# State products of two sample streams in two row halves of the array, their parts laid out through memory

## The chip, the core and the metric

The kernel is one program on one core of a Trainium2 chip. The metric is the device time of one execution in microseconds (us), lower is better. TensorE is the matrix engine (PE; its weight loads are listed as PEld), VectorE is DVE, ScalarE is ACT, GpSimd is POOL, and SyncE (SP) only issues transfers here. Products go to PSUM, which the kernel uses as 8 banks of 128 x 512 numbers.

## The reference, cut to what matters

One layer of a streaming encoder: a half-step FFN, a mixer (short convolution, and retention with four heads), a second half-step FFN. It runs over 512 frames of one new stream and over 16 frames of each of 8 running streams ("sample streams"). The part that the change touches is the new state of each sample stream: for each head, S_new = decay * S + k^T v, where k is 16 frames x 256, v is 16 frames x 512 and S is 256 x 512.

```python
k_dec = k * jnp.exp(lg[None, :] * (L - 1.0 - idx[:, None]))[None, :, :, None]
S_new = jnp.exp(lg * L)[None, :, None, None] * S + jnp.einsum('blhd,blhe->bhde', k_dec, v)
```

## The kernel before

Products are made in float32r from a high and a low part of each operand, in three products: low x high, high x low, high x high. The 640 rows of activations (512 new, 128 sample) run as tiles of 128. Each engine has its program in order; semaphores tie them together. PSUM banks are handed out round robin: `bank(n)` on PE waits until the banks that it will write have been freed (`psum_free`, counted up by DVE or ACT when they have read a bank), and `psum_full` tells the readers.

A head (`head(i)` on each engine, i = 0 to 3) is, on PE: the v and k projections (`natural(4, ...)`), transposes of the rotated keys, scores, `cross(0)` (products of a query with the old states, in four column groups of the array), the output tiles, a gate unit (`unit_of_chunk`), transposes of the normalised output, `cross(1)`, the new state of the long stream, the transposes of the sample rows (banks from U_T5 on), and then the state products of the sample streams in three places: `state_products(1, (0, 1))` ahead of the output projection, `state_products(1, (2, 3))` after its first quarter (m = 0), and `state_products(0, range(4))` at its end, right ahead of the next head's projections. I call the three places A, B and C.

The sample keys of all 8 streams are one tile of 128 rows (16 rows a stream), with parts k4h and k4l; the values are v4h and v4l. ACT copies them into `vp` and `kp` (`pack`, lines 1618 to 1622): group g of four holds two streams, in rows 0 to 31 the high part, 32 to 63 one low part, 64 to 95 the high part again, so that one product of 96 rows gives all three. Rows 96 to 127 are zeroed once (lines 2271, 2272). As one group holds two streams, ACT makes for each stream a copy `km` of the keys with the other stream's rows set to zero (`masked_keys`, lines 1624 to 1629, factor `odd_even`), four ahead of place A and four behind place B. A stream takes two products of 128 x 128 by 128 x 512 (`state_products`, lines 1237 to 1246), 16 in a head.

The order of the work around it. DVE: the gated output of the sample rows (`gated(4)`, `gated(5)`) frees the last two of the banks that the output projection's `bank(4)` at m = 0 waits for; `new_state` (line 2394) adds each product to the state and frees its bank; `branch(m)` takes the output projection's banks. ACT: after `kd` it packs, waits for `packed`, makes the gate's sigmoid, `gated_hi`, the root of the variance. SP (`head_loads`, line 658): after `cross(0)` it loads the second four states into `state`, waits for `packed`, and loads `swish` into `sg`, whose memory v4h and v4l share; DVE's `gated(0)` waits for that load. After it come the next weight chunks. POOL loads the high parts of weight chunks and splits off the low ones.

Of the kernel before, what the change touches and what calls it, by code (L numbers as in the profile page):

```python
# [8 lines left out]
NP, NS_, TS = 512, 8, 16  # L9
# [160 lines left out]

HT_S, HT_M, HT_Q, HT_K, HT_G, HT_W = 0, 512, 640, 768, 773, 776
# [121 lines left out]
def build_layer(nc, a):  # L293
# [3 lines left out]
    with ctx:  # L297
# [3 lines left out]
        def sem(name):  # L301
            return ctx.enter_context(nc.semaphore(name))
# [18 lines left out]
        odd_even = sb("odd_even", [128, 2])  # L321
# [7 lines left out]
        slab = (nc.sbuf_base + 31) // 32 * 32  # L329
        end = nc.sbuf_base + nc.sbuf_bytes_remaining  # L330
# [69 lines left out]
        km = hm.take("km", [128, 4, DK], f32r)  # L400
        SC0 = [0, 512, 896, 1152, 1280]
        rot_at = hm.at
# [77 lines left out]
        packed = sem("packed")  # L480
        keys_masked = sem("keys_masked")
# [81 lines left out]
        def _(sync):  # L563
# [94 lines left out]
            def head_loads(i):  # L658
# [5 lines left out]
                sync.wait_ge(packed, i * 24 + 12)  # L664
                sync.dma_start(sg[:, 0:SWISH_TILES, :], a["swish"][i]).then_inc(swish_in, 16)
# [146 lines left out]
        def _(pe):  # L812
            ck, bk, hr, zr, hd, kc = (Count() for _ in range(6))
# [423 lines left out]
            def state_products(group, slots):  # L1237

                for bb in slots:
                    kc.add()  # L1240
                    pe.wait_ge(keys_masked, kc())
                    for d in range(2):
                        b = bank()
                        last = mm(ps[:, b, :], km[:, bb, d * 128:(d + 1) * 128],
                                  vp[:, (4 * group + bb) // 2, :], True, True)
                    last.then_inc(psum_full, 2)
# [19 lines left out]
            def head(i):  # L1266
# [48 lines left out]
                state_products(1, (0, 1))  # L1315
                assert bk.at - u0 == U_OUT

                for m in range(4):
# [11 lines left out]
                    if m == 0:  # L1330
                        state_products(1, (2, 3))
                state_products(0, range(4))
# [12 lines left out]
            pe.wait_ge(consts_in, 32)  # L1345
# [12 lines left out]
        def _(act):  # L1358
# [49 lines left out]
            def window(ffn):  # L1408
# [25 lines left out]
                if ffn == 0:  # L1434
                    act.dma_start(ident[:, :], a["ident"]).then_inc(consts_in, 16)
                    act.dma_start(odd_even[:, :], a["odd_even"]).then_inc(consts_in, 16)
# [129 lines left out]
            act.wait_ge(consts_in, 32)  # L1566

# [50 lines left out]
            def pack(out, n, part):  # L1618

                for g in range(4):  # L1620
                    copy(out[32 * n:32 * n + 32, g, :], part[32 * g:32 * g + 32, :].bitcast(f32)
                         ).then_inc(packed, 1)

            def masked_keys(group):

# [13 lines left out]
            def head(i):  # L1639
# [46 lines left out]
                for n in range(4):  # L1686
                    gated_hi(n)
# [925 lines left out]
```

## Time and profile before

| | us |
|---|---|
| median of 3 runs | 1798.13 |
| the 3 runs | 1797.13 to 1800.16 |
| the profiled execution | 1800.08 |
| its span | 1798.3 |
| PE busy in the span | 1775.9 (99%) |
| DVE, ACT, POOL busy | 1282.8, 647.9, 547.0 |
| TensorE clock granted, mean | 0.998 |

The four heads run from about 943 to 1296 us of the span. In a timeline row the first number is the start, the second the time from the start of the first to the end of the last of the instructions merged in it. Products overlap in the records: a product of 128 x 512 is listed with 0.39 us, but in a dense row one starts every 0.227 us, and this pitch is what it costs.

### The profile page before, as it was taken

Reading aid. Unit: us, or ns where it says so; the run is one execution under the profiler, and the core shown is the slowest. Engines: PE = TensorE matmul, PEld = TensorE weight load, DVE = VectorE, ACT = ScalarE, POOL = GpSimd, SP = SyncE. Lnnn points to the kernel's source line nnn. Section 1 sums busy time; section 2 is a strip of 40 time slices with the busy share of each in tenths; the row PEclk is TensorE's granted clock in tenths of the full one; section 3 lists DMA queues with packets and bytes.
Section 4 is the critical chain, followed back from the end, with each engine's and each line's share of the span. In section 5 each row is a group of like instructions: output and inputs, shape, how many; then the busy total and the mean of one; then the engine's idle time right before and its main releaser. Section 6 shows DMA issues by size and latency. Waiting matters only on the chain.

```text
span 1798.3 us, 26938 instructions
## 1 busy us (share of the span) xinstructions
PE 1775.9 (99%) x10852; PEld 1654.3 (92%) x10852; DVE 1282.8 (71%) x1694; ACT 647.9 (36%) x1105; POOL 547.0 (30%) x361
## 2 busy tenths in 40 slices
PE   9999999999999999999999999999999999999997
PEld 8989999898999999999998979797988989899895
DVE  7958485678788787776257666767867958485675
ACT  5425233242545454543106050504224425243242
POOL 2424242242232222221341323232243324233231
PEclk9999999999999999999999999999999999999999
DMA  7442424324443343432864959586972342423313
GB/s 272 132 138 71 141 79 133 119 94 175 147 147 126 112 138 98 141 102 76 292 225 153 338 187 328 189 296 233 345 273 95 129 141 71 139 73 129 128 48 105
DMA packets 88986, 285.74 MB, mean 159 GB/s; under 512 B 8736, under 2 KB 11168, under 8 KB 88608
## 3 DMA queue, kind: packets, MB, share of 16 engines
q1 hardware_dynamic: 48176, 171.72, 28.9%
q0 software_dynamic: 15120, 55.06, 9.1%
q10 hardware_dynamic: 25568, 57.26, 8.7%
q8 instruction: 86, 1.41, 0.3%
q14 instruction: 36, 0.29, 0.1%
HBM read 242.78 MB, written 42.28 MB: 159 GB/s over the span
## 4 chain that ended last, share of the span: by engine, by line
PE 96%; DVE 1%; DMA 1%; issue 1%; ACT 0%; POOL 0%; DVEq 0%; SPq 0%; POOLq 0%; ACTq 0%
PE ps L818 95%; PE ps L1227 1%; DMA wh<-in_weights 1%; PE ps L1136 0%; DMA raw<-in_weights 0%; DVE y L2192 0%; POOL wl L720 0%; ACT xh L1367 0%; DVE ct L1795 0%; DVE z L2181 0%; DVE y L2201 0%; DVE hl L1795 0%; DVE wl L1795 0%; ACT hh L1367 0%; DVE rt L1795 0%
## 5 line engine op out<-in xcount | busy, mean ns | idle before, releaser
L818 PE MATMUL ps<-th,wql 128*128 128x320 f32 x1136 | 350.9, 309 | 0.0
L818 PE MATMUL ps<-th,wqh 128*128 128x320 f32 x1136 | 350.7, 309 | 0.0
L818 PE MATMUL ps<-tl,wqh 128*128 128x320 f32 x1136 | 350.1, 308 | 0.0
L720 POOL TENSOR_TENSOR wl<-raw,wh 128x1024 fp32r<-128x1024 f32 x101 | 259.8, 2573 | 104.0 <-DMA wh<-in_weights 69.1
L1367 ACT ACTIVATE pu<-ps 128x320 f32<-128x320 f32 x213 | 93.3, 438 | 526.4 <-PE ps L818 526.3
L1795 DVE TENSOR_TENSOR wql<-qraw,wqh 128x512 fp32r<-128x512 f32 x213 | 263.3, 1236 | 17.3 <-ACT wqh L1367 17.1
L818 PE MATMUL ps<-xl,wqh 128*128 128x320 f32 x852 | 262.7, 308 | 0.0
L818 PE MATMUL ps<-xh,wqh 128*128 128x320 f32 x852 | 262.7, 308 | 0.0
L818 PE MATMUL ps<-xh,wql 128*128 128x320 f32 x852 | 262.6, 308 | 0.0
L733 POOL TENSOR_TENSOR quad_s<-qraw 128x512 f32<-128x512 f32 x71 | 93.6, 1318 | 473.1 <-DVE wql L1795 425.9
L1795 DVE TENSOR_TENSOR wql<-quad_s,wqh 128x512 fp32r<-128x512 f32 (+1 forms) x213 | 194.2, 912 | 46.1 <-ACT wqh L1367 45.3
L708 POOL DMA_DIRECT2D wh<-in_weights x99 | 55.7, 563 | 525.0 <-PE ps L818 419.8
L818 PEld LDWEIGHTS ps<-tl,wqh 128*128 128x128 f32 x1136 | 213.3, 188 | 0.4
L818 PEld LDWEIGHTS ps<-th,wql 128*128 128x128 f32 x1136 | 213.2, 188 | 0.4
L818 PEld LDWEIGHTS ps<-th,wqh 128*128 128x128 f32 x1136 | 213.3, 188 | 0.0
L1367 ACT ACTIVATE wqh<-quad_s 128x512 fp32r<-128x512 f32 (+1 forms) x213 | 163.7, 769 | 50.2 <-PE ps L818 50.2
L818 PE MATMUL ps<-wh,hl 128*128 128x512 f32 x430 | 168.3, 391 | 2.0 <-issue 1.4
L818 PE MATMUL ps<-wh,hh 128*128 128x512 f32 x430 | 167.6, 390 | 0.0
L818 PE MATMUL ps<-wl,hh 128*128 128x512 f32 x430 | 167.6, 390 | 0.0
L818 PEld LDWEIGHTS ps<-xh,wql 128*128 128x128 f32 x852 | 159.9, 188 | 0.6 <-issue 0.2
L818 PEld LDWEIGHTS ps<-xl,wqh 128*128 128x128 f32 x852 | 160.0, 188 | 0.4
L818 PEld LDWEIGHTS ps<-xh,wqh 128*128 128x128 f32 x852 | 160.0, 188 | 0.0
(224 smaller groups left out, 3429.7 us busy)
## 6 DMA issues: line engine op xcount, KB each, us to landing
qraw<-in_quads SPq DMA_DIRECT2D x142, 512.0 KB, 3.7
raw<-in_weights SPq DMA_DIRECT2D x105, 512.0 KB, 3.8
wh<-in_weights POOLq DMA_DIRECT2D x99, 512.0 KB, 5.2
state<-in_state_ret ACTq DMA_DIRECT2D x32, 512.0 KB, 7.1
out_ret_sample<-state ACTq DMA_DIRECT2D x32, 512.0 KB, 4.5
state<-in_state_ret SPq DMA_DIRECT2D x16, 512.0 KB, 5.4
qk_scratch<-ctp SPq DMA_DIRECT2D x8, 640.0 KB, 5.5
swish_scratch<-ctp SPq DMA_DIRECT2D x6, 640.0 KB, 3.0
```

Source lines behind the costliest of these rows:

```text
L708: pool.dma_start(w_hi(r), a["weights"][c]).then_inc(hi_loaded[r], 16)
L720: pool.tensor_tensor(w_lo(r), w_raw(r), w_hi(r).bitcast(f32), ALU.subtract).then_inc(chunk_split, 1)
L733: pool.tensor_tensor(qs[:, 0, :], qraw[:, c0, 512:1024], qraw[:, c1, 512:1024], ALU.add).then_inc(pool_sums, 1)
L818: ins = nc.tensor.matmul(out, lhs, rhs, start=start, stop=stop, skip_group_check=adds)
L1227: last = nc.tensor.transpose(cols(k, 128, ps[:, b, :]), src, ident[:, :])
L1367: return nc.scalar.activation(out, in_, ACT.Copy, **kw)
L1795: return V.tensor_tensor(out, x, y, op)
```

## The change

The state products of a group g now run from `vp` and `kp` themselves, without a mask. The two streams of a group no longer lie interleaved: the even stream's three parts of 16 rows fill rows 0 to 47, the odd stream's rows 64 to 111. A product has 48 rows, in the lower or upper half of the array. The count stays at 16 a head, each with 128 x 512 results, in the order even, odd for each half d of the keys. A call does one group and takes its four banks at once. The places stay: g = 2 at A, g = 3 at B, g = 0 and 1 at C.

As no engine but a transfer moves rows freely, the parts go through memory: ACT issues six transfers a head, which store v4h, v4l, v4h and k4h, k4h, k4l into `packed_values` and `packed_keys` (16-row blocks side by side for each stream); SP issues four that load them into the two halves of `vp` and `kp`. The 24 copies of `pack`, the 8 of `masked_keys`, the table `odd_even` and the two memsets go. PE waits for the loads, ACT and SP for the stores. `slab` is padded so that its distance to `xh` stays at three quarters of LEVEL, and the buffers behind `kp` move.

```diff
+PACKED, PACK_STORES, PACK_LOADS = 3 * TS, 16 * 3, 16 * 2
...
-        odd_even = sb("odd_even", [128, 2])
...
+        slab += (3 * LEVEL // 4 - (slab - xh_at)) % LEVEL
...
-        km = hm.take("km", [128, 4, DK], f32r)
+        hm.at = max(hm.at, sums_at + 8 * KT * NT)
...
-                sync.wait_ge(packed, i * 24 + 12)
-                sync.dma_start(sg[:, 0:SWISH_TILES, :], a["swish"][i]).then_inc(swish_in, 16)
+                for out, of, saved, done in ((vp, "packed_values", values_saved, values_packed),
+                                             (kp, "packed_keys", keys_saved, keys_packed)):
+                    sync.wait_ge(saved, PACK_STORES * (i + 1))
+                    for odd in range(2):
+                        sync.dma_start(out[64 * odd:64 * odd + PACKED, :, :].bitcast(f32),
+                                       a[of].rearrange("(g o) p d -> o p g d", o=2)[odd]).then_inc(done, 16)
+                    if out is kp:
+                        continue
+                    sync.dma_start(sg[:, 0:SWISH_TILES, :], a["swish"][i]).then_inc(swish_in, 16)
...
-            def state_products(group, slots):
-
-                for bb in slots:
-                    kc.add()
-                    pe.wait_ge(keys_masked, kc())
-                    for d in range(2):
-                        b = bank()
-                        last = mm(ps[:, b, :], km[:, bb, d * 128:(d + 1) * 128],
-                                  vp[:, (4 * group + bb) // 2, :], True, True)
-                    last.then_inc(psum_full, 2)
+            def state_products(i, g):
+
+                b0 = bk.at
+                bank(4)
+                pe.wait_ge(values_packed, PACK_LOADS * (i + 1))
+                pe.wait_ge(keys_packed, PACK_LOADS * (i + 1))
+                for d in range(2):
+                    for odd in range(2):
+                        rows = slice(64 * odd, 64 * odd + PACKED)
+                        last = mm(ps[:, (b0 + 2 * odd + d) % 8, :], kp[rows, g, d * 128:(d + 1) * 128],
+                                  vp[rows, g, :], True, True)
+                last.then_inc(psum_full, 4)
...
-                state_products(1, (0, 1))
+                state_products(i, 2)
...
-                        state_products(1, (2, 3))
-                state_products(0, range(4))
+                        state_products(i, 3)
+                for g in range(2):
+                    state_products(i, g)
...
-            def pack(out, n, part):
-
-                for g in range(4):
-                    copy(out[32 * n:32 * n + 32, g, :], part[32 * g:32 * g + 32, :].bitcast(f32)
-                         ).then_inc(packed, 1)
-
-            def masked_keys(group):
-
-                for bb in range(4):
-                    st = 4 * group + bb
-                    copy(km[:, bb, :], kp[:, st // 2, :].bitcast(f32),
-                         scale=odd_even[:, st % 2:st % 2 + 1]).then_inc(keys_masked, 1)
+            def save_packed(out, parts, saved):
+
+                for n, part in enumerate(parts):
+                    act.dma_start(out[:, TS * n:TS * n + TS, :], part[:, :].bitcast(f32)).then_inc(saved, 16)
...
-                pack(vp, 0, v4[0])
-                pack(vp, 1, v4[1])
-                pack(vp, 2, v4[0])
+                if i:
+                    act.wait_ge(values_packed, PACK_LOADS * i)
+                save_packed(a["packed_values"], (v4[0], v4[1], v4[0]), values_saved)
                 act.wait_ge(k4_made, i + 1)
-                pack(kp, 0, k4[0])
-                pack(kp, 1, k4[0])
-                pack(kp, 2, k4[1])
+                if i:
+                    act.wait_ge(keys_packed, PACK_LOADS * i)
+                save_packed(a["packed_keys"], (k4[0], k4[0], k4[1]), keys_saved)
...
-                act.wait_ge(packed, i * 24 + 12)
+                act.wait_ge(values_saved, PACK_STORES * (i + 1))
...
+                act.wait_ge(keys_saved, PACK_STORES * (i + 1))
                 for n in range(4):
                     gated_hi(n)
                 roots(5, 6)
-                act.wait_ge(packed, i * 24 + 24)
-                masked_keys(1)
...
-                act.wait_ge(psum_full, u0 + U_S1B + 4)
-                masked_keys(0)
...
-            step(V.memset(vp[96:128, :, :].bitcast(f32), 0.0))
-            step(V.memset(kp[96:128, :, :].bitcast(f32), 0.0))
```

## Rows read from the trace of the kernel before

**Rows 1.** The page: the chain that ended last, by engine.
```profile
PE 96%; DVE 1%; DMA 1%; issue 1%; ACT 0%; POOL 0%; DVEq 0%; SPq 0%; POOLq 0%; ACTq 0%
```

**Rows 2.** Groups by line and shape (busy us, mean ns | idle before): state products.
```profile
L818 PE MATMUL ps<-vp,km 128*128 128x512 f32 x64 | 17.1, 399 | 0.0
```

**Rows 3.** Timeline of PE and DVE at place A, first head.
```profile
982.84 1.17 PE L818 MATMUL ps<-vp,km 128*128 128x512 f32 x4
983.05 0.74 DVE L1795 TENSOR_TENSOR ogt<-ps,sg 128x256 f32<-128x256 f32 x2
...
983.89 0.39 PE L818 MATMUL ps<-ogh,wl 128*128 128x320 f32 x1
```

**Rows 4.** Timeline of PE at place B, first head.
```profile
991.01 1.09 PE L818 MATMUL ps<-vp,km 128*128 128x512 f32 x4
991.94 0.31 PE L818 MATMUL ps<-ogh,wl 128*128 128x320 f32 x1
```

**Rows 5.** Timeline of PE and DVE at place C, first head.
```profile
1013.06 2.02 PE L818 MATMUL ps<-vp,km 128*128 128x512 f32 x8
1013.33 0.82 DVE L2409 COPY z<-ps 128x640 f32<-128x640 f32 x1 [1.35 <-PE ps L818]
...
1014.07 2.06 DVE L2400 SCALAR_TENSOR_TENSOR state<-state,ht,ps 128x512 f32<-128x512 f32 x3
...
1014.95 0.47 PE L818 MATMUL ps<-wh,xl 128*128 128x512 f32 x1
```

**Rows 6.** Timeline of PE around the first head's first `cross`, in four column groups.
```profile
954.72 0.28 PE L818 MATMUL ps<-ql,kh 128*128 128x256 f32 x1
954.84 0.28 PE L818 MATMUL ps<-qh,kh 128*128 128x256 f32 x1
955.04 1.92 PE L818 MATMUL ps<-state,qx 128*32 128x512 f32 x16
956.79 1.04 PE L818 MATMUL ps<-vs,sc 128*32 128x512 f32 x8
957.76 0.50 PE L818 MATMUL ps<-vh,scl 128*128 128x512 f32 x1
958.09 0.39 PE L818 MATMUL ps<-vl,sch 128*128 128x512 f32 x1
```

**Rows 7.** Timelines of ACT and DVE, first head, from packing to the gate.
```profile
951.98 2.58 ACT L1367 ACTIVATE vp<-v4h 32x512 fp32r<-32x512 f32 x4
...
968.48 1.28 ACT L1674 ACT_TABLE_LOAD   x1 [1.88 <-PE ps L818]
...
956.96 0.42 DVE L1795 TENSOR_TENSOR k4l<-kd,k4h 128x256 fp32r<-128x256 f32 x1
...
972.83 1.28 DVE L1795 TENSOR_TENSOR ogt<-ps,sg 128x512 f32<-128x512 f32 x2
```

**Rows 8.** Timeline of SP's queue, first head.
```profile
957.89 1.92 SPq L662 DMA_DIRECT2D state<-in_state_ret  x4
959.85 0.75 SPq L665 DMA_DIRECT2D sg<-swish_scratch  x1
972.05 41.76 SPq L571 DMA_DIRECT2D raw<-in_weights  x5
```

**Rows 9.** Transfers of the stretch 950 to 985 us, 40 slices; landing in us.
```profile
GB/s 169 257 407 346 19 0 0 0 0 0 56 220 389 396 403 403 413 417 430 334 80 0 9 0 0 0 122 248 403 365 61 0 0 0 0 0 0 0 0 0
...
sg<-swish_scratch SPq DMA_DIRECT2D x1, 960.0 KB, 10.3
```

**Rows 10.** Last head: SP's queue, DVE, and the transfer in 1237 to 1257.
```profile
1240.87 0.47 SPq L665 DMA_DIRECT2D sg<-swish_scratch  x1
...
1253.85 1.28 DVE L1795 TENSOR_TENSOR ogt<-ps,sg 128x512 f32<-128x512 f32 x2
...
sg<-swish_scratch SPq DMA_DIRECT2D x1, 960.0 KB, 9.4
```

**Rows 11.** The page: small stores to memory, issue to landing.
```profile
out_y_sample<-y SPq DMA_DIRECT2D x2, 256.0 KB, 3.2
```

More of the change, by code:

```diff
@@ L479, in build_layer @@
         head_ready = sem("head_ready")
-        packed = sem("packed")
-        keys_masked = sem("keys_masked")
+        values_saved, keys_saved = sem("values_saved"), sem("keys_saved")
+        values_packed, keys_packed = sem("values_packed"), sem("keys_packed")
         swish_sig_made, swish_made, swish_in, k4_made = (
@@ L812, in _ @@
         def _(pe):
-            ck, bk, hr, zr, hd, kc = (Count() for _ in range(6))
+            ck, bk, hr, zr, hd = (Count() for _ in range(5))
             owed = [False]
@@ L1344, in _ @@
             ffn(True)
-            pe.wait_ge(consts_in, 32)
+            pe.wait_ge(consts_in, 16)
             begin_stage()
@@ L1435, in window @@
                     act.dma_start(ident[:, :], a["ident"]).then_inc(consts_in, 16)
-                    act.dma_start(odd_even[:, :], a["odd_even"]).then_inc(consts_in, 16)
                     act.dma_start(convw[:, :, :], a["conv_w"]).then_inc(cache_in, 16)
@@ L1565, in _ @@
             roots_and_to_T(1)
-            act.wait_ge(consts_in, 32)
             def state_load(i):
@@ L2589 @@
         "ident": np.eye(128, dtype=np.float32),
-        "odd_even": ((np.arange(128)[:, None] // TS % 2 == np.arange(2)[None, :])
-                     & (np.arange(128)[:, None] < 96)).astype(np.float32),
     }
@@ L2603 @@
     for name, shape in (("qk", (H, 2, 128, 2, NT)), ("swish", (H, 128, SWISH_TILES, NT)), ("gate_c", (128, KT, NT)), ("gate_r", (128, KT, NT)),
-                        ("mix", (128, KT, NT))):
+                        ("mix", (128, KT, NT)), ("packed_values", (NS_, PACKED, DV)), ("packed_keys", (NS_, PACKED, DK))):
         args[name] = nc.dram_tensor(f"{name}_scratch", shape, mybir.dt.float32, kind="Internal").ap()
```

## The prediction

> **What bounds the kernel now.** I read the chain first: TensorE carries 96% of it [rows 1]. So a saving counts only where PE starts its next product earlier, and a cost only where PE is made to wait. ACT, which the change relieves of 32 copies a head, is not on the chain, and I give that relief nothing. Next the group of the products that change: 64, no idle time ahead of them [rows 2]. Then the timeline at the three places of a head, to see what releases the work that follows.
>
> Place A: four products start at 982.84; the output projection starts at 983.89 [rows 3]. At the dense pitch of 0.227 us four would end at 983.75. The rest is a wait for DVE: it needs the banks that `gated(4)` and `gated(5)` free, and these two run from 983.05 to 983.79. DVE sets that start.
>
> Place B: 991.01 to 991.94 is 0.93 us for four, 4 x 0.227 = 0.91 and no wait [rows 4]. PE sets it.
>
> Place C: eight from 1013.06, the next head's first product at 1014.95 [rows 5]. Eight pitches are 1.82, to 1014.88. The first bank of the next head must be freed by DVE: `branch(7)` runs 1013.33 to 1014.15, and the first of the three state updates of 2.06 us ends at about 1014.07 + 0.74 = 1014.81; a semaphore's tenth later is 1014.92. PE and DVE end there together. The other three heads repeat this to within 0.05 us, as they do at A and B.
>
> **The change, part by part.**
>
> The pairs. Two products in different row halves ought to run side by side. The trace has no row halves, but it has column quarters: 24 products of `cross`, each listed at 0.59 us, start 16 of them in 956.79 - 955.04 = 1.75 us, four each 0.44 us [rows 6]. Four quarters overlap fully there. So I take a pair at one pitch of 0.227; the bounds are 0.22 (a quarter product's 0.109 twice) and 0.454 (one behind the other).
>
> The switch of the array's shape. Around `cross`: the score product before it starts at 954.84, pitch 0.12, so the next was due at 954.96 and came at 955.04: 0.08. After it, the second four of `vs,sc` began at 957.22 and were due to hand over at 957.66; the next came at 957.76, and its successor 0.33 later where 0.227 is usual: 0.10 + 0.10 [rows 6]. I take 0.28 for a visit; the bounds are 0 and 0.56 (a row switch twice as dear). The Trainium skill (TensorEngine Tiling, Key Properties) says that changing the tiling mode drains the engine; the trace agrees with these 0.28 us. By that page's speedup of up to two, without its drain, place B would gain 0.45 instead of what follows.
>
> Place A: 982.84 + 0.08 + 2 x 0.227 + 0.10 = 983.48, before the 983.86 at which DVE lets the projection go. Gain 0. All of the saved time becomes wait.
>
> Place B: 0.08 + 0.454 + 0.20 = 0.73 against 0.93: gain 0.20, bounds +0.48 (no switch cost) and -0.08 (double). `bank(4)` here wants two banks more at once, those of the first two streams' state; DVE updates that state right after place A, some 7 us of projection earlier, so they are free.
>
> Place C: group 0 ends at about 1013.06 + 0.08 + 0.45 = 1013.6. Group 1 takes its four banks at once, so it waits for `branch(7)`, 1014.15 + 0.07 = 1014.22, where before only its last stream did. It ends at 1014.22 + 0.45 + 0.10 = 1014.77, and the next head still waits for DVE until 1014.92. Gain 0, cover left 0.15. With that cover gone each 0.1 us more costs 0.4 in the sum.
>
> Transfers instead of copies. Values are stored from 951.98 on, three issues of 256 KB [rows 7]; 256 KB land in 3.2 us elsewhere [rows 11], so all are in memory near 957.5, before SP has issued its state loads (957.89 to 959.81) [rows 8]. Keys are ready when k4l is made, 957.38 [rows 7], and land some 5 us later. ACT's two new waits end long before the gate (968.48) and `gated_hi`, which follows `gated(0)` at 972.83 [rows 7]; behind them only these two wait. SP's wait for the keys has the next weight load behind it, issued at 972.05 in any case [rows 8]. The loads of `kp` queue behind `sg` and should land near 974, 8 us before PE asks.
>
> What is not free is that `sg` now stands behind the loads of `vp` in SP's queue. In the first head it is issued at 959.85 and lands 10.3 later, at 970.15 [rows 8, 9]; DVE needs it at 972.83 [rows 7]. Margin 2.7 us. In the last head 1240.87 + 9.4 = 1250.3 against 1253.85: 3.6 [rows 10]; the middle two have 4.2. The stretch moves 403 GB/s when full [rows 9]; ahead of `sg` now come 0.79 MB of `vp` and, on ACT's queue, up to 0.39 MB of keys: 1.18 MB / 403 GB/s = 2.9 us. So `sg` is late by 0.2 us in the first head and in time in the others. From `gated(0)` to place A, DVE is busy nearly without a gap and PE waits for it, so what is late there is paid in full. Bounds: 0 (the keys use the idle stretch before 959) and 1.8 in all (0.4 MB/us plus one more issue of 0.75 us: 3.9 us late gives 1.2 + 0.3 + small ones).
>
> Addresses: `slab` stays at its level; `sc`, `on`, `rot` move 1184 bytes down, level 0 instead of 160. 64 `vs,sc` products see that. I take 0, bounds +-0.6 us (0.01 us each). Both memsets lie in a stretch where DVE waits for PE: 0.
>
> Sum: 4 x (0 - 0.20 + 0) + 0.2 = -0.6 us. The profiled execution took 1800.08 (span 1798.3 and 1.8 around it), so it would be 1799.5. It stands 1.95 above the median of the three; against the median, which is what will be compared, 1798.13 - 0.6 = **1797.5 us**.
>
> **The rivals.**
>
> R1, the halves do not run side by side, so that the change does not do what it says. Then A ends 982.84 + 0.08 + 0.91 + 0.10 = 983.93, +0.07; B 1.19 against 0.93, +0.26; C 1014.22 + 0.91 + 0.10 = 1015.23, +0.31. That is 0.64 a head, 2.6 in four, with `sg` 2.8: 1800.9. For it: no row product in the trace. Against it: the column quarters, whose weight loads start together too.
>
> R2, slower: the swish load becomes the bound. Place: SP's queue ahead of `gated(0)`. With a delay d in each head, the loss is (d - 2.7) + 2 (d - 4.2) + (d - 3.6); it makes the kernel slower by 0.2% from d = 4.75 on. At d = 5.4 it is 6.9 less 0.8: 1804.2. For that the new transfers would have to cost nearly twice their bytes at 403 GB/s, or the values' stores would have to land after SP asks at 959.8. The Trainium skill (DMA: Bandwidth & Descriptors, Why a DMA increments its semaphore by 16) says that a transfer uses only as many engines as divide both slowest dimensions: 8 streams against 128 partitions gives 8 of 16 engines for the six stores. No row before the change has such a store. What speaks for R2 in rows is the margin of 2.7 us only.
>
> R3, DVE's hold at A and C is softer than I read it, and the pairs count everywhere: 32 pitches of 0.227 less 12 visits of 0.28, -3.9: 1794.2. Against it: both holds are dependences in the code with ends that match within 0.1 us.
>
> **How the numbers follow.** Forecast 0.62, R1 0.14, R2 0.10, R3 0.05; the remaining 0.09 I leave to what I have not seen (addresses, transfers that collide elsewhere), two thirds of it slower. The measurement tells about 0.2% from no change, 3.6 us. Forecast and R1 are inside it, R2 above 1801.7, R3 at its edge. Faster 0.06, same 0.81, slower 0.13. The runs alone spread by 1.5 us around their middle; the range takes in the forecast, its bounds (-1.9 to +2.1 with place B's and the load's ends) and R1: 1795.2 to 1801.4.
>
> **What would show it.** In the profile after: pairs of products starting within a few hundredths in A, B and C (if one starts each 0.227, R1); B's first product to the next projection's 0.73; an unchanged 1.05 at A and 1.89 at C with the wait put down to DVE; `sg` landing about 2.9 us later after its turn; no PE wait for `vp` or `kp`. A DVE wait for `sg` ahead of `gated(0)` of more than a few tenths in every head would be R2. The prediction is wrong if a head gains or loses more than 0.9 us, or if something outside the heads moves by more than 1 us.

## The result and the profile after

The kernel after takes 1821.65 us (median of 4 runs, 1820.46 to 1825.82) beside 1798.68 for the kernel before on the same chip (4 runs, 1797.13 to 1800.16). The ratio is 1.0129, 95% interval 1.0117 to 1.0141: slower by 1.3%, where 1797.5 was forecast and 1801.4 was the top of the range. Its span is 1819.0 us, 20.7 more than before, and the mean granted clock 0.995 (0.998 before). Medians and ratios here and below are of runs near full clock: two of e16's ten runs (1935 and 2498 us, at granted clocks of 0.85 and 0.65) are left out.

The page of the kernel after, the chain by engine and TensorE's busy time, to be held against [rows 1]:

```profile
PE 82%; issue 5%; DMA 4%; DVE 3%; POOL 2%; SPq 1%; ACT 0%; DVEq 0%; POOLq 0%; ACTq 0%
PE 1780.5 (98%) x10852; PEld 1652.5 (91%) x10852; DVE 1285.2 (71%) x1692; ACT 585.3 (32%) x977; POOL 547.5 (30%) x361
```

TensorE has fallen from 96% of the chain to 82%, and transfers with their issues have taken most of the difference. The answer for the tile `sg` (what its engine sat idle for, us and times, and the time from issue to landing) and TensorE's waits (total, times, longest) say which transfer:

```profile
  DMA sg<-swish_scratch: 19.4, 4
...
DMA to landing us min/median/max: 13.8/16.2/17.7
```

```profile
PE ps L1235 <- DVE on L2270: 16.3, 4, 5.9
```

DVE waits once a head for the load of `swish`, 19.4 us in all, and TensorE then waits for DVE's normalised output, 16.3 us in all. Before, this load landed in 8.2 to 10.3 us and DVE never waited for it. DVE's timeline at `gated(0)` in the first three heads shows the size of each wait, in brackets:

```profile
978.40 1.29 DVE L1792 TENSOR_TENSOR ogt<-ps,sg 128x512 f32<-128x512 f32 x2 [4.66 <-DMA sg<-swish_scratch]
...
1079.96 1.29 DVE L1792 TENSOR_TENSOR ogt<-ps,sg 128x512 f32<-128x512 f32 x2 [6.68 <-DMA sg<-swish_scratch]
...
1177.62 1.29 DVE L1792 TENSOR_TENSOR ogt<-ps,sg 128x512 f32<-128x512 f32 x2 [3.47 <-DMA sg<-swish_scratch]
```

The last head's is 4.6. The first transpose of the rotated keys in each head slips against before by 0.8, 5.8, 13.5 and 16.1 us, and the stage behind the heads by 21.3. So the four heads lose 5.0, 7.7, 2.7 and 5.1, 20.5 in all; 0.8 is lost ahead of them and 0.6 regained behind.

TensorE idles for 16.3 of these 20.5 us; DVE makes up for some 0.8 of each of its own waits before TensorE needs it. The other 4.2 us go with TensorE's clock. Its wait in the second head, and then, for each head, the stretch from the first transpose behind the wait (`ident,on`) to the first product of the output projection; the third number from the end is the granted clock:

```profile
1088.30 1.97 PE L1235 MATMUL ps<-ident,on 128*128 128x128 f32 x8 [5.91 <-DVE on L2270]
...
986.74:989.75 3.01, 3.01 (x12) 2.03 (x12) 2.43 (x6) 0.83 (x2) 0.00 (x0) 0.51 0.00 0
1088.30:1091.35 3.05, 3.05 (x12) 2.07 (x12) 2.46 (x6) 0.83 (x2) 0.00 (x0) 0.50 0.00 0
1185.96:1187.86 1.90, 1.76 (x12) 1.18 (x13) 1.80 (x4) 0.40 (x2) 0.00 (x0) 1.00 0.00 0
1283.06:1285.45 2.39, 2.39 (x12) 1.41 (x13) 2.24 (x6) 0.75 (x2) 0.00 (x0) 0.65 0.99 401
```

Before, the stretch took 1.90 us in every head, at a clock of 1.00. In the first, second and fourth head, ahead of which TensorE had idled 3.88, 5.91 and 3.85 us, the clock fell to its lower level of 1.2 GHz (0.50) for all or part of the stretch, which took 3.01, 3.05 and 2.39 us: 2.7 us lost. In the third, after an idle time of 2.67 us, it stayed at 2.4 GHz and nothing was lost. The remaining 1.4 us or so are what is left over; the projection's products right behind account for them at least in part: in the second head they start each 0.27 us up to 1092.6, where 0.15 is usual. In e1, e4, e11, e16 and e18 below, in whose profiled heads no wait for `sg` is over 1.2 us, the clock stays at its full level through all four heads.

SP's queue in the first head, after (start, time to the end of the last issue):

```profile
958.71 2.21 SPq L663 DMA_DIRECT2D state<-in_state_ret  x4
960.96 1.31 SPq L669 DMA_DIRECT2D vp<-packed_values_scratch  x2
962.31 0.51 SPq L673 DMA_DIRECT2D sg<-swish_scratch  x1
...
966.89 0.80 SPq L669 DMA_DIRECT2D kp<-packed_keys_scratch  x2
```

Against [rows 8] `sg` is issued 2.5 us later: 0.8 because the state loads start later, most of the rest for the two new issues. It then lands 16.1 us after its issue where it took 10.3 [rows 9]. These 5.8 us are the part that has to be explained. The transfers of 950 to 985 us, after (40 slices of 0.875 us, issues with their landing):

```profile
GB/s 0 154 342 398 321 119 157 115 166 169 143 104 276 366 397 377 394 408 371 166 178 273 255 297 201 197 183 232 200 315 315 286 225 220 210 98 5 0 0 0
...
sg<-swish_scratch SPq DMA_DIRECT2D x1, 960.0 KB, 16.1
vp<-packed_values_scratch SPq DMA_DIRECT2D x2, 384.0 KB, 11.5
```

Two stretches are slow. From 954.4 to 960.5 us, slices 6 to 12, the stores run at 104 to 169 GB/s in a stretch that was empty before. From 966.6 us on, the 20th slice, `vp` comes in: 166 and 178 GB/s, and not over 315 from there to the end, where the kernel before moved 403 to 430. In the records of the single packets a 2 KB packet takes 84 ns up to 966 us and 130 to 200 after it, and `swish`'s packets of 7.5 KB take 492 ns on average in the four heads, 297 before. From 966.6 us on the engines are listed as full; each packet takes longer.

TensorE's side, first head, place B (after):

```profile
996.97 0.30 PE L826 MATMUL ps<-ogh,wh 128*128 128x320 f32 x1
997.20 0.73 PE L826 MATMUL ps<-vp,kp 48*128 48x512 f32 x4
997.86 0.41 PE L826 MATMUL ps<-ogh,wl 128*128 128x320 f32 x1
998.12 0.31 PE L826 MATMUL ps<-ogl,wh 128*128 128x320 f32 x1
```

and place C:

```profile
1018.95 0.31 PE L826 MATMUL ps<-ogh,wh 128*128 128x320 f32 x1
1019.18 0.73 PE L826 MATMUL ps<-vp,kp 48*128 48x512 f32 x4
1020.24 0.73 PE L826 MATMUL ps<-vp,kp 48*128 48x512 f32 x4 [0.32 <-DVE z L2404]
1020.99 0.47 PE L826 MATMUL ps<-wh,xl 128*128 128x512 f32 x1
```

Four products take 0.66 us to their successor at B (0.93 before, [rows 4]): pairs do run side by side. At C the second four wait for DVE, and the last product ahead of them to the next head's first is 2.04 us, as before. At both places the four products take what was forecast to within 0.1 us; what the switch of shape costs behind them is weighed under e7 and e8. The 23 us are lost in the transfers.

### The profile page after: what moved, and what is told of

It reads as the page before. It is cut to its first block, busy times and chain, and to the rows that moved or that the text cites. A ratio compares the mean times of both kernels' runs of the same rounds, so it can differ in the third digit from the quotient of the medians.

```text
span 1819.0 us, 26808 instructions
## 1 busy us (share of the span) xinstructions
PE 1780.5 (98%) x10852; PEld 1652.5 (91%) x10852; DVE 1285.2 (71%) x1692; ACT 585.3 (32%) x977; POOL 547.5 (30%) x361
## 4 chain that ended last, share of the span: by engine, by line
PE 82%; issue 5%; DMA 4%; DVE 3%; POOL 2%; SPq 1%; ACT 0%; DVEq 0%; POOLq 0%; ACTq 0%
PE ps L826 82%; DMA sg<-swish_scratch 3%; POOL wl L728 2%; DMA wh<-in_weights 1%; DVE ogl L1792 0%; PE ps L1235 0%; PE ps L1144 0%; DVE z L1792 0%; SPq L663 0%; POOL wh L716 0%; DVE y L2189 0%; ACT xh L1378 0%; DVE ogt L1792 0%; DVE ct L1792 0%; DVE z L2178 0%
```

## The experiments

Diffs are against the kernel after unless said. The kernel before ran beside each: 1798.60 (e1 to e4), 1799.38 (e5 to e8), 1798.97 (e9 to e11), 1798.84 (e12 to e14), 1798.47 (e15 to e18).

### Is it the queue's order, the loads or the stores?

**e1: `swish` ahead of the loads.**

```diff
+                sync.wait_ge(values_saved, PACK_STORES * (i + 1))
+                sync.dma_start(sg[:, 0:SWISH_TILES, :], a["swish"][i]).then_inc(swish_in, 16)
                 for out, of, saved, done in ((vp, "packed_values", values_saved, values_packed),
...
-                    sync.dma_start(sg[:, 0:SWISH_TILES, :], a["swish"][i]).then_inc(swish_in, 16)
```

> The changed kernel with one edit: SP issues the swish load ahead of the loads of vp and kp instead of between them. My theory now: nearly all of the 20.7 us in the span is DVE waiting for sg ahead of gated(0), 19.4 us in four waits, and PE after it. Then sg lands within 12 us of its issue at about 961, DVE waits under 1 us in all, and the time is 1797 to 1801. Rival: the product halves or the new waits on PE cost something of their own, or the later loads of kp only move the wait: then it stays above 1805.

1800.40 us, ratio 1.0006 (0.9997 to 1.0016), `sg` waits 1.4 us in two heads. The transfers of 950 to 985 in e1:

```profile
GB/s 37 164 379 435 227 159 166 150 190 176 62 229 254 364 390 394 404 434 419 437 400 180 154 238 236 180 185 198 158 149 288 193 276 229 98 0 0 0 0 0
```

The loss is gone, so it came through the wait for `sg` alone. The slow stretch is not gone: it now stands behind `swish`, at 149 to 288 GB/s, with `vp` and `kp` in it and nobody waiting. The loads themselves are slow, not `swish` behind them.

**e2 and e3: one side left out after the first head.**

```diff
-                    for odd in range(2):
+                    for odd in range(2 if i == 0 else 0):
```

```diff
-                save_packed(a["packed_values"], (v4[0], v4[1], v4[0]), values_saved)
+                if i == 0:
+                    save_packed(a["packed_values"], (v4[0], v4[1], v4[0]), values_saved)
```

> Left out: in heads 1 to 3 the loads of vp and kp; their products use head 0's values. The six stores of each head stay. If the stores are what holds sg up (8 of 16 engines busy with them up to 959.7 us, then keys beside the state loads): sg still lands 13 us or more after its issue in heads 1 to 3 and the time stays above 1812. If the loads are: DVE waits some 5 us for sg in head 0 and under 1 us in the others, 1801 to 1806.

> Left out: in heads 1 to 3 the six stores; the loads of vp and kp stay and read what head 0 stored. If the loads hold sg up: sg lands 14 us or more after its issue in heads 1 to 3, DVE waits 3 to 6 us a head, 1814 to 1821. If the stores do: a wait in head 0 alone, 1801 to 1806.

e2, without loads in heads 1 to 3: 1806.66 us, 1.0032 (1.0018 to 1.0045); `sg` waits once, 4.0 us in the first head, and lands in 9.8 and 9.9 us in the others. Its runs spread from 1802.41 to 1807.37, and the profiled one, with a span of 1800.6, is among the shortest; so I read from it where it waits, not how much is left. e3, without stores in heads 1 to 3: 1811.52, 1.0063 (1.0046 to 1.0080), waits 13.6 us, among them 5.22 and 2.05 in the heads without stores. In the profiled execution stores alone delay nothing; its median says that typical runs lose some 4 us more, and no trace shows where. Loads alone cost most of it: 9.2 us of waits in heads 1 to 3, where the kernel after has 14.8.

**e6: stores on all engines.** The six stores write one block of 128 rows each, in place of 8 streams x 16 rows.

```diff
-                    act.dma_start(out[:, TS * n:TS * n + TS, :], part[:, :].bitcast(f32)).then_inc(saved, 16)
+                    act.dma_start(out.rearrange("s p d -> (s p) d")[128 * n:128 * n + 128, :], part[:, :].bitcast(f32)).then_inc(saved, 16)
```

> The changed kernel, but each of the six stores writes its 128 rows to 128 rows of memory side by side, so that nothing in its shape is 8; the loads are unchanged and so bring rows that are not theirs. If the stores ran on 8 of 16 engines (share 0.47 and 160 GB/s from 954 to 959 us): they finish in half the time and the key stores no longer load one half of the engines; then sg lands 1 to 3 us earlier than in the changed kernel, 1810 to 1817. If the stores cost only their bytes: no change, 1820 to 1823.

1811.65 us, 1.0071 (1.0056 to 1.0086). The transfers of 950 to 985 in e6:

```profile
GB/s 0 131 318 332 344 377 405 190 0 0 169 229 138 384 403 405 412 405 391 204 150 152 180 198 171 361 404 293 174 232 281 346 375 56 23 0 0 0 0 0
```

The stores now run at 318 to 405 GB/s and are through by 957, where the kernel after had them at 104 to 169 until 960. So half of the engines is what they use there: in the records of after the 16 engines are busy 0.47 on average while the values are stored. The Trainium skill (DMA: Bandwidth & Descriptors, Why a DMA increments its semaphore by 16) gives 8 of 16 engines for this shape; these runs agree. The loads that follow are as slow as before (150 to 204). Waits for `sg` come to 8.8 us in three heads, and in the first DVE starts at 977.23, just as `sg` lands, after 3.5 us put down to a product that had long ended: 12.3. The half stores thus take some 10 us of the 23, but only together with the slow loads: with them the four state loads land in a median of 8.0 us in that stretch instead of 5.7 in e6, which eats into the margin of 2.7 to 4.2 us that hides the stores in e2.

### What makes the loads slow?

**e4: the same bytes into 128 partitions.** As many bytes, packets and issues, the products read what lies in their rows.

```diff
-                        sync.dma_start(out[64 * odd:64 * odd + PACKED, :, :].bitcast(f32),
-                                       a[of].rearrange("(g o) p d -> o p g d", o=2)[odd]).then_inc(done, 16)
+                        sync.dma_start(out[:, (0, 1)[odd]:(1, 3)[odd], :].bitcast(f32),
+                                       a[of].rearrange("s p d -> (s p) d").rearrange("(g q) d -> q g d", q=128)[:, (0, 1)[odd]:(1, 3)[odd], :]).then_inc(done, 16)
```

> The loads of vp and kp move the same bytes in the same 2 KB and 1 KB rows from the same stores, but into 128 partitions (3 groups) instead of 48 at a time; the products read rows that are not theirs. If the loads are slow because each is packed into 48 partitions (the 2 KB packets took 130 to 204 ns from 966 us on, against 85 ns for those of the state loads): packets at 85 ns again, sg lands 10 to 12 us after its issue, 1798 to 1804. If they are slow because of what they read (rows just written to memory, a stride between groups) or because of the stores: no change, 1815 to 1822.

1799.61 us, 1.0003 (0.9993 to 1.0012), no wait for `sg`, landing 10.3 to 10.7. The transfers of 950 to 985 in e4:

```profile
GB/s 94 229 407 379 197 180 190 199 176 47 102 266 236 372 377 392 407 397 407 417 431 408 376 379 200 170 98 314 389 365 33 0 0 0 0 0 0 0 0 0
```

Slices 19 to 22 now hold 407 to 431 GB/s. The whole loss is gone with the stores as they were: it is the shape of the loads.

**e5, e9, e10: 48 rows spread out, sixteen rows apart and together.**

```diff
-                        sync.dma_start(out[64 * odd:64 * odd + PACKED, :, :].bitcast(f32),
+                        sync.dma_start(out[odd:odd + 2 * PACKED - 1:2, :, :].bitcast(f32),
```

```diff
+                    for n in range(6):
...
+                        sync.dma_start(out[n:n + 121:8, :, :].bitcast(f32),
...
+                        sync.dma_start(out[16 * n:16 * n + 16, :, :].bitcast(f32),
```

(the last two lines are e9's and e10's)

> The changed kernel, each load of vp and kp still 48 partitions from the same rows of memory in the same order, but into every second partition (0, 2, .. 94 and 1, 3, .. 95) instead of 48 in a row; rows 96 to 127 zeroed once; the products read rows that are not theirs. If what is slow is the crowding of the writes into 48 neighbouring partitions: the 2 KB packets fall from some 150 to 220 ns to about 90, sg lands 10 to 12 us after its issue, 1798 to 1803. If it is what the loads read in memory, or that a load has only 48 partitions: unchanged, 1815 to 1822.

> The changed kernel with each of vp and kp loaded by six transfers of 16 partitions, eight apart (n, n + 8, ... n + 120), the same bytes from the same rows; vp and kp zeroed once; the products read rows that are not theirs. Theory: a load's rate goes with how many groups of 8 neighbouring partitions it writes: 48 in a row touch 6 of 16 (in the run with the swish load first they ran alone at about 140 GB/s, against 390 to 400 of full ones), 48 of 96 touch 12 (about 290). So here, 16 of 16, the packets stay near 85 to 95 ns; sg is issued 2 to 3 us later for the four more issues and lands some 10 us after, DVE waits 0 to 2 us a head, 1799 to 1806. Rival: small loads are slow because they have few partitions: then worse than the changed kernel, over 1825.

> The same as e9_sixteen_apart but each transfer into 16 neighbouring partitions (16n to 16n + 15), 2 groups of 8 of 16. Theory: the 0.79 MB of vp move at some 50 GB/s, 15 us instead of 2, sg lands 25 us or so after its issue and DVE waits some 10 us a head: 1835 to 1865. Rival: as in e9 the number of transfers or of partitions is what counts, and the two runs take the same time.

e5: 1811.15 us, 1.0060 (1.0040 to 1.0080), waits 8.8 (its runs spread from 1804.23 to 1813.05, and the profiled one took 1806.77). e9: 1814.11, 1.0083 (1.0069 to 1.0097), waits 13.0. e10: 1836.31, 1.0208 (1.0194 to 1.0222), waits 31.1. The transfers of 950 to 985 in e10:

```profile
GB/s 56 206 445 407 178 183 190 171 159 101 74 242 307 400 363 394 404 403 206 143 112 117 225 138 155 173 134 142 136 140 342 172 180 226 268 346 263 118 187 28
```

Same rows, same issues, and e10 loses 22 us more than e9: where the partitions lie decides. Spreading them does not restore the pace either: e9 shows 194 to 245 GB/s in slices 19 to 22, and its packets of 2 KB take 157 ns at 967 to 968 us. But its 13 us are not all pace. Its six issues put `sg` into the queue 2.6 to 3.3 us later in a head than the two of e4 do, and outside the first head `sg` then lands 10.6 to 11.5 us after its issue, nearly as in e4. My expectation for e9 (1799 to 1806) was missed by 8 us, and I could not say from these three whether it is crowding, or few partitions, or both.

**e12 to e14: the order of the rows in memory.** e12 fills 128 partitions from rows that lie close together in memory, e13 the 48 partitions of the kernel after and e14 the sixteen apart of e9 from rows that lie far from each other.

```diff
+                                       a[of].rearrange("s p d -> (s p) d").rearrange("(g j e) d -> g e j d", e=16, j=8)[g]
...
+                                       a[of].rearrange("s p d -> (s p) d").rearrange("(p g o) d -> o p g d", g=4, o=2)[odd]).then_inc(done, 16)
...
+                                       a[of].rearrange("s p d -> (s p) d").rearrange("(p g n) d -> n p g d", g=4, n=6)[n]
```

> The wide loads of e4 (128 partitions, 3 groups), but the rows of memory are dealt so that the 16 engines read neighbouring rows, 2 KB apart, instead of each its own block of 16 KB; one transfer a group. If only the destination counts: 1798 to 1803, packets near 90 ns. If the closeness of the rows read counts: packets of 120 ns and more, 1806 to 1816.

> The changed kernel's loads into 48 partitions in a row, twice, but each partition's four rows lie in a block of eight rows of its own, so that neighbouring engines read 48 KB apart. If the rows read count: sg lands some 3 us earlier than in the changed kernel, 1808 to 1815. If only the destination counts: 1818 to 1823.

> e9 (sixteen partitions eight apart, six transfers), but the 16 engines read rows 48 KB apart instead of 2 KB. If the rows read are what kept e9 slow: packets near 90 ns, 1800 to 1806. If not: 1812 to 1816 as e9, and then what e9 shares with e5 and not with e4 is the small number of partitions.

e13: 1823.01 us, 1.0134 (1.0119 to 1.0149), waits 19.7, as the kernel after. e14: 1811.62, 1.0077 (1.0062 to 1.0092), waits 11.7, near e9. e12: 1802.02, 1.0019 (1.0009 to 1.0028), waits 5.2; its slices 19 to 22 hold 273 to 327 GB/s, and its packets of 2 KB take 103 ns at 967 to 968 us, 85 in e4. So reading rows that lie close together costs a little, and reading them far apart wins back nothing of the 23 us.

**e15 to e18: sets of partitions.** Here I formed the theory that comes nearest: the 128 partitions fall into 16 sets of 8, each set four neighbours and the four that lie 32 above them; a transfer goes at the pace of its fullest set. The Trainium skill (SBUF — State Buffer, Door 1: The DMA port swizzle) describes such sets as ports. e15 and e16 have equal issues, partitions and packets, e17 and e18 are the same block of 64 neighbours with another start.

```diff
+                    for n in range(3):
+                        sync.dma_start(out[(0, 1, 64)[n]:(63, 64, 127)[n]:2, :, :].bitcast(f32),
...
+                        sync.dma_start(out[n:n + 125:4, :, :].bitcast(f32),
...
+                    sync.dma_start(out[0:64, :, :].bitcast(f32),
...
+                    sync.dma_start(out[32:96, :, :].bitcast(f32),
```

(one line of destination each, for e15, e16, e17 and e18)

> The values and the keys are loaded in three transfers each, of 32 partitions and all four column blocks: rows 0, 2, .. 62, then 1, 3, .. 63, then 64, 66, .. 126. The products read what lies in their rows, so the new states are not those of the reference; bytes, packets and products are as many as in the kernel after. Theory of sets: the 128 partitions form 16 sets of 8 (four neighbours and the four 32 above them), each with a sixteenth of the 400 GB/s that full stretches show, and a transfer lasts as long as its fullest set. It gives for the 48 neighbouring rows of the kernel after 8 of 48 rows in the fullest set, 150 GB/s (seen: 166 to 178 at first), for every second of 96 rows 4 of 48, 300 (seen: 235 to 317), for sixteen rows 8 apart 2 of 16, 200, for sixteen together 4 of 16, 100 (seen with two in flight: 112 to 173). Here 4 of 32 rows: 200 GB/s, though no two rows of a transfer are neighbours. Swish waits 9 to 15 us, time 1808 to 1815. Neighbourhood: like e5_spread_rows or better, waits 6 to 9 us, since the rows lie as far apart as there. Number of partitions: fewer than 48, so waits over 9 us here and as many in e16. The Trainium skill (SBUF - State Buffer, Door 1: The DMA port swizzle) describes such sets as ports.

> As e15_second_of_half, but the three transfers take every fourth partition of all 128: rows 0, 4, .. 124, then 1, 5, .. 125, then 2, 6, .. 126. The new states are not those of the reference here either. Theory of sets: 2 of 32 rows in each of the 16 sets, 400 GB/s as for a load into 128 partitions; what is left is the third issue, so as e12_wide_close_rows: swish waits 0 to 5 us, time 1798.5 to 1802.5. Neighbourhood: between e5_spread_rows (every second) and e9_sixteen_apart (every eighth), waits 8 to 13 us, 1809 to 1814. Number of partitions: as e15, over 9 us.

> The values and the keys are loaded in one transfer each, into 64 neighbouring partitions from 0 on, four column blocks: two thirds of the bytes of the kernel after, and the new states are not those of the reference. Theory of sets: 8 of 64 rows in the fullest set, 200 GB/s, so 512 KB take 2.6 us where they would take 1.3 at 400; packets of 2 KB take about twice the 85 ns that they take in the state loads. Swish lands 1.3 us or more later than in e18; waits of a few tenths to 2 us in the first head, time 1798.5 to 1803. Neighbourhood and number of partitions: no difference from e18 in packets, rate or landing.

> As e17_sixty_four_from_0, but the block of 64 neighbouring partitions begins at 32; the new states are not those of the reference. Theory of sets: 32 to 63 fill eight sets with four rows each, 64 to 95 the eight others: 4 of 64 rows, 400 GB/s, packets of 2 KB near 85 to 100 ns, swish lands 1.3 us or more earlier than in e17 and no wait; time 1797.5 to 1800.5. Neighbourhood and number of partitions: as e17 in all.

e15: 1829.83 us, 1.0174 (1.0159 to 1.0189). e16: 1799.98, 1.0009 (0.9999 to 1.0019). e17: 1821.25, 1.0127 (1.0112 to 1.0142). e18: 1799.32, 1.0005 (0.9996 to 1.0015). The transfers of 950 to 985 and what waited for `sg`, e15:

```profile
GB/s 89 206 398 379 199 176 150 171 185 138 78 234 303 400 369 396 399 407 180 140 138 154 221 219 193 208 156 172 294 166 191 203 255 263 318 233 180 66 5 0
...
  DMA sg<-swish_scratch: 25.7, 4
```

e16, where nothing waited for `sg`:

```profile
GB/s 37 220 384 393 234 159 173 190 192 112 57 214 248 356 362 372 376 410 396 414 418 421 408 376 246 198 124 164 370 435 173 0 0 0 0 0 0 0 0 0
```

e17:

```profile
GB/s 0 178 300 407 314 176 183 157 187 169 57 147 282 365 376 356 400 403 350 147 145 147 203 276 200 252 280 157 142 322 300 231 276 215 84 0 0 0 0 0
...
  DMA sg<-swish_scratch: 17.4, 4
```

e18, again without a wait:

```profile
GB/s 23 206 342 398 279 173 194 185 190 96 50 180 277 403 361 365 392 399 384 434 387 434 368 270 179 16 33 197 346 407 215 0 0 0 0 0 0 0 0 0
```

The reader looks at slices 19 to 22 in each. Sixty-four neighbours from 0 run at 145 to 147 GB/s once the stretch has turned, sixty-four from 32 at 384 to 434. Every second partition of a half is as slow as neighbours are (138 to 180), every fourth of all 128 runs at 396 to 421. Neither neighbourhood nor number does that: e15 is spread and slow, e18 is crowded and fast, and both pairs have equal numbers. In the packet records of 967 to 968 us, 2 KB take 254 ns in e15, 243 in e17, 84 in e16 and 89 in e18.

All the loads of the study in this light, with the rate by sets of a full 400 GB/s:

| loads | rows in the fullest set | GB/s by sets | GB/s seen, first slices | ratio |
|---|---|---|---|---|
| e10, 16 together | 4 of 16 | 100 | 112 to 143 | 1.0208 |
| after, 48 in a row | 8 of 48 | 150 | 166 to 178 | 1.0129 |
| e13, 48 in a row, far rows | 8 of 48 | 150 | 169 to 194 | 1.0134 |
| e15, second of half | 4 of 32 | 200 | 138 to 154 | 1.0174 |
| e17, 64 from 0 | 8 of 64 | 200 | 145 to 147 | 1.0127 |
| e9, 16 apart | 2 of 16 | 200 | 194 to 245 | 1.0083 |
| e14, 16 apart, far rows | 2 of 16 | 200 | 206 to 318 | 1.0077 |
| e5, second of 96 | 4 of 48 | 300 | 235 to 246 | 1.0060 |
| e16, every fourth | 2 of 32 | 400 | 396 to 421 | 1.0009 |
| e18, 64 from 32 | 4 of 64 | 400 | 384 to 434 | 1.0005 |
| e4, 128 | 8 of 128 | 400 | 407 to 431 | 1.0003 |
| e12, 128, close rows | 8 of 128 | 400 | 273 to 327 | 1.0019 |

The loads that fill all 16 sets alike are the fast ones, e12 being slowed by the rows that it reads. The fullest set does not give the pace, nor even the order: e15 and e17, put at 200 GB/s, run at 138 to 154, below the 48 in a row that are put at 150, and my expectations of them (up to 1815 and 1803) were missed by 15 and 18 us. The ratios hold more than the pace, since the issues and TensorE's clock add to them: in e15, as in e10, the clock is at 1.2 GHz for 6.8 us in each head. What is shown is that the same bytes in as many packets are fast when they are shared out over all the sets and slow when they lie in half of them. Why half of the sets gives a third of the pace and not half stays open, and that a set is made of four neighbours was not varied by itself.

### TensorE's ledger

**e7 and e8**, on e4, where no wait for `sg` blurs it: all products in rows 0 to 47 (none side by side), and products over all 128 rows (no switch).

```diff
-                        rows = slice(64 * odd, 64 * odd + PACKED)
+                        rows = slice(0, PACKED)
```

```diff
+                        rows = slice(0, 128)
```

> The run with the wide loads (transfers out of the way), but all state products read rows 0 to 47, so that no two lie in different halves. If pairs in different halves overlap: here four products take 4 x 0.227 instead of 2 x 0.227, so place B takes some 0.45 us more, A about 0.1 more, C 0.4 more, 3 to 4 us in all against the wide loads (1799.6), 1802 to 1804. If they never overlapped: the same time as the wide loads to 0.5 us.

> The run with the wide loads, but all state products read all 128 rows: no row halves, no switch of the array's shape, four banks at once as in the change. Against e7_same_half this is the price of the switch: place B 0.93 us as before the change and no gap of 0.2 us around it; place C still waits for DVE before its second four. I expect 0.2 to 0.3 us less than same_half in each of the places that PE sets, 1800 to 1802.5.

e7: 1804.25 us, 1.0029 (1.0019 to 1.0039). e8: 1800.26, 1.0005 (0.9995 to 1.0014). TensorE at place B in e4, in halves:

```profile
991.09 0.30 PE L826 MATMUL ps<-ogh,wh 128*128 128x320 f32 x1
991.33 0.73 PE L826 MATMUL ps<-vp,kp 48*128 48x512 f32 x4
991.99 0.41 PE L826 MATMUL ps<-ogh,wl 128*128 128x320 f32 x1
992.24 0.31 PE L826 MATMUL ps<-ogl,wh 128*128 128x320 f32 x1
```

in e7, one half:

```profile
991.56 0.30 PE L826 MATMUL ps<-ogh,wh 128*128 128x320 f32 x1
991.79 1.19 PE L826 MATMUL ps<-vp,kp 48*128 48x512 f32 x4
992.91 0.41 PE L826 MATMUL ps<-ogh,wl 128*128 128x320 f32 x1
```

and in e8, all rows:

```profile
990.82 0.31 PE L826 MATMUL ps<-ogh,wh 128*128 128x320 f32 x1
990.97 1.08 PE L826 MATMUL ps<-vp,kp 128*128 128x512 f32 x4
991.89 0.31 PE L826 MATMUL ps<-ogh,wl 128*128 128x320 f32 x1
992.03 0.31 PE L826 MATMUL ps<-ogl,wh 128*128 128x320 f32 x1
```

From the last product ahead to the first behind: 0.90 in halves, 1.35 in one half, 1.07 without a switch. So pairing saves 1.35 - 0.90 = 0.45, two pitches of 0.227, and the switch costs 1.35 - 1.07 = 0.28. One more piece shows a row later: the successor comes after 0.25 us in halves, after 0.14 in e8 (992.24 - 991.99 and 992.03 - 991.89). With these 0.11 place B gains 1.07 - 0.90 - 0.11 = 0.06 us a head.

**e11: a version for use.** Streams padded to 64 rows in memory, so that one load fills 128 partitions, and `swish` ahead of it. (`stored(i)` counts one more store in the first head, which fills the padding.)

```diff
+                    sync.dma_start(out[:, :, :].bitcast(f32),
+                                   a[of].rearrange("(g o) p d -> (o p) g d", o=2)).then_inc(done, 16)
...
-                        ("mix", (128, KT, NT)), ("packed_values", (NS_, PACKED, DV)), ("packed_keys", (NS_, PACKED, DK))):
+                        ("mix", (128, KT, NT)), ("packed_values", (NS_, ROWS_KEPT, DV)), ("packed_keys", (NS_, ROWS_KEPT, DK))):
```

> A correct version that takes both findings: each stream's rows in memory are padded from 48 to 64, so that vp and kp are each loaded by one transfer into all 128 partitions (a third more bytes; the padding is stored once), and SP issues the swish load ahead of them. Theory: sg lands 10 to 11 us after its issue, DVE waits nowhere, what is left is the gain of the halves at place B, 0.06 us a head: 1797 to 1800, not to be told from before. Rival: the stores on half of the engines and the extra bytes still cost 1 us or more.

1799.23 us, 1.0003 (0.9994 to 1.0012), no wait for `sg`, landing 9.7 to 10.5. The change can be had without its loss, but there is nothing under it to win.

## Why the prediction was wrong

**The step that failed** is the price of what stands ahead of `sg`: "1.18 MB / 403 GB/s = 2.9 us". The 403 was read from a stretch in which every transfer fills all 128 partitions [rows 9], and it was applied to loads of 48 and to stores by half of the engines, of which the trace had no row. The loads moved at 166 to 178 GB/s. In the first head `sg` landed at 962.31 + 16.1 = 978.4, 8.3 us later than before, not 2.9. The bound I gave, one more issue and 0.4 MB/us, was no bound (and its terms give 3.7 us, not 3.9): it held the rate fixed, and the rate was the unknown. The stores were mis-sized in the same way: "all are in memory near 957.5" came from another store's 3.2 us, and here the stretch of the stores lasts to 960.5 at 104 to 169 GB/s.

**R2 is what happened.** Its place, its formula and its sign were right: with d = 8.3 it gives (8.3 - 2.7) + 2 (8.3 - 4.2) + (8.3 - 3.6) = 18.5 us, and DVE waited 19.4. That they agree so well is partly luck. The 8.3 us are the first head's and hold 0.8 us by which the whole kernel was already late; counted from the start of its own head, `sg` was late by 7.4, 10.9, 7.7 and 8.2 us, each head's wait plus its margin. And the formula charges the wait to TensorE in full and its clock at nothing: TensorE idled 16.3 us, and its lower clock in three heads cost 4.2 more. Its chance of 0.10 and its example of d = 5.4 were too low. The rule that I named beside it, half of the engines for the stores, agrees with the rows and yet is the lesser half: it explains none of the waits alone (e2's profiled execution), and some 10 us beside the loads (e6 against after). What mattered, the sets of partitions that a load fills, I did not weigh.

**The margins** of 2.7, 4.2, 4.2 and 3.6 us were read right and are why the costs do not add: of the 7.4 to 10.9 us in a head 3.5 to 6.7 show as a wait.

**Pairs**: a pair was put at one pitch of 0.227, and four products save two pitches, 0.45, shown by e7 against e4. **R1** did not happen; made on purpose it costs 4 to 5 us against e4 (1.0029 against 1.0003), where the sum had 2.6 + 0.8. By rows of a head against e4: at A 2.15 instead of 1.90 from the transposes to the projection, 0.25 where I had 0.07; at B 0.45, or 0.28 against the kernel before, where I had 0.26; at C 2.43 instead of 2.04, 0.39 where I had 0.31. That is 1.09, four times 4.4.

**The switch**: 0.28 around the visit, as forecast, and 0.11 more on the product behind the first successor. Place B gains 0.06 a head and not 0.20. This was mis-sized by 0.14 a head, 0.6 in the kernel, too little to be seen in a time.

**Place A** gains nothing: 1.90 us from the transposes to the projection in before, e4, e8 and the one head of after in which the clock did not fall. **Place C** gains nothing: 2.04 in before and after, with the wait for DVE where it was forecast, ahead of the second four. In e8, whose products take the old time but in the new grouping of banks, the same distance is 2.33, and the product behind comes 0.08 us sooner: the four banks at once cost 0.21, which is R1's 0.31 without its 0.10 for the switch, and the pairs just pay for them.

**ACT's relief** from 647.9 to 585.3 us busy bought nothing, as forecast. **R3** did not happen. **Addresses and memsets**: e4 has them all and stands at 1.0003. The 0.8 us that the kernel after loses before the first head's transposes I have not explained; e4 is 0.2 us late at `gated(0)`.

## What to carry to other kernels

A rate read from a trace belongs to the shape it was read from: before a copy by an engine is replaced with a transfer, ask which partitions each new transfer fills and whether they are shared out evenly over sets of four neighbours with the four 32 above, and give the rate a range of its own if no row shows that shape. 32 to 95 is as good as all 128, 0 to 63 is not; and a store whose outer dimension is 8 uses half of the engines. Then look at what stands behind the new transfer in its queue and how many microseconds of margin that has, since a slow transfer with nobody behind it costs nothing (e1). And a wait of TensorE can cost more than its length: look at the granted clock of the products behind it.

## What the runs showed of the hardware

- Loads from memory into half of the sets of partitions ran at a third of the full pace: 145 to 147 GB/s for 64 partitions from 0 (e17) against 384 to 434 for 64 from 32 (e18), 2 KB packets 243 ns against 89. The DMA engines are listed as full in both; a busy share says nothing of the pace here.
- Transfers that share the time with such a load slow down too: `swish`, which fills all partitions, has packets of 492 ns in the kernel after and 297 before.
- Two float32r products of 48 rows in different row halves ran entirely side by side (four took 0.90 us where e7's took 1.35); a visit of four of them cost 0.28 us for the switch of shape and 0.11 more behind it, so four products barely pay for it.
- After idle times of 3.88, 5.91 and 3.85 us TensorE's granted clock was at 1.2 GHz and a stretch of 1.90 us took up to 3.05; after one of 2.67 us it was at 2.4 GHz and the stretch took 1.90.
